# Last down projection of a two-block network: eight subtractions of its activation sums move from VectorE to GpSimd

## The chip, the cores and the metric

The program runs on one core of one Trainium2 chip. The metric is its device time in microseconds (us); the time before is 1531.18 us, the median of three runs (1530.91 to 1531.45). One core has five engines that work side by side, each in the order of its own program: TensorE (PE), VectorE (DVE), ScalarE (ACT), GpSimd (POOL) and SyncE (SP, which here only starts transfers). They wait for each other by semaphores.

## What is computed

Two residual blocks one after the other, on 512 tokens of width 1024, all in float32. What matters here is the end of the second block, a gated feed-forward layer and its last product:

```
h2 = rmsnorm(x, g_ffn)
x = x + (silu(h2 @ w_ff_gate) * (h2 @ w_ff_up)) @ w_ff_down
return rmsnorm(x, g_final)
```

`w_ff_down` is 2816 x 1024. That last product is the "down projection"; the feed-forward layer of the first block has one too, by another procedure that the change leaves alone.

## The kernel before

**Numbers in two parts.** The kernel keeps a float32 value as a high part (type fp32r, rounded) and a low part (value minus high part). A product of two such values is three matmuls: high by high (L1060), high weight-low by high (L1063), high weight by low activation (L1064), all added up in PSUM. Four of these triples, one per block of 128 rows, make what is below called one form. ScalarE rounds to the high part (all by line L1615), VectorE or GpSimd subtracts to get the low part.

**Strassen-like products.** The down projection has 22 row blocks of 128. Its first part, "standard tiles" (`std_tile`, units 0 to 3 in `STD_UNITS`, 512 tokens wide), runs plainly on panels of weights that GpSimd splits (`std_split`, L1004, L1005, L1007). Row blocks 0 to 15 of the other output tiles go by seven products of half size instead of eight (`strassen_unit`, forms F1 to F7, each 256 tokens wide). Six such units follow (unit 0 to 5 below), with standard tiles between some of them. TensorE takes the forms of a unit in the order F1, F6, F7, F5, F2, F3, F4.

**Sums of weights.** For each unit GpSimd makes two sums (`add5` L914, `add7` L923) and the low parts of F1, F7, F2 and F4 (`form_lo_of`, L932). VectorE makes `add6` (L2451), `add3` (L2456) and the low parts of F6, F5, F3 (L2462). ScalarE copies a sum to PSUM (`sum_copy`, L1807) and makes all the high parts.

**Sums of activations.** Before unit 0 the sums of activations must be made, once, for eight k (0 to 7), while TensorE is still on the standard tiles. For each k, ScalarE copies two activations into PSUM (`down_copies`, L2137 and L2138), VectorE adds their low parts (`down_parts`, three instructions L3016 to L3018, the first of which writes the small buffer `down_t1(k)`) and makes four sums (`down_t_sums`, five instructions L3025 to L3029). Three sums stand in PSUM and serve F6, F7, F4: ScalarE rounds them (`down_token_hi`), VectorE subtracts (`down_lo`, L3035). The fourth stands in `down_t1(k)` and serves F5: ScalarE rounds it over the activation itself (`down_token_late`), and VectorE subtracts (`down_late`, L3041, 128x256, both inputs in SBUF). These eight are the late sums of the title of the change.

**What ties them.** `down_t1(k)` is `tmp[:, k % 4 // 2, HALVES[k % 2]]`: four halves of two tiles for eight k. So `down_parts(k)` for k of 4 and more waits until the late low part of k - 4 is made (L3015). `down_parts(5)` also waits for ScalarE's copies of k = 5, which wait for `down_lo(3)`. `sum_copy` of unit 0 waits for `down_lo(5)` (L1802), and so does F1 of unit 0 on TensorE (L1371). F5 of units 0 and 1 waits for the late parts 0 to 3 and 4 to 7, one per triple (L1385). F1 of unit 2 waits for `v`, the third of the joins L3053, L3056, L3059 of the products of units 0 and 1.

**The order of the work** is written out by hand per engine: `down_dve` on VectorE, `pool_down` on GpSimd, `down_act` on ScalarE, `down_strassen` on TensorE. A `std_split` waits on GpSimd until TensorE has begun the panel before (`panel_used`). Low parts of activations, late or not, all count on one semaphore, `t_ready`, in the order `T_ORDER`.

Of the kernel before, what the change touches and what calls it, by code (L numbers as in the profile page):

```python
# [22 lines left out]
KT = D // P  # L23
# [19 lines left out]
QUAD = 4  # L43
# [61 lines left out]
LOADED = 16  # L105
# [132 lines left out]
def build(nc, t, out):  # L238
# [5 lines left out]
    with ctx:  # L244
# [590 lines left out]
        def _(pool):  # L835
# [173 lines left out]
            def pool_down(f):  # L1009

                unit = [pair_of(3 + f, n) for n in range(6)]

                def forms(n, more=None):
                    for form in (F1, F7, F2):
                        form_lo_of(form, unit[n])
                    if more is not None:
                        add5(unit[more])
                        add7(unit[more])
                    form_lo_of(F4, unit[n])

                for u in range(3):
                    for s in range(PAIR):
                        std_split(f, u, s)
                std_split(f, 3, 0)
                add5(unit[0])
                std_split(f, 3, 1)
                add7(unit[0])
                forms(0, 1)
                forms(1, 2)
                forms(2, 3)  # L1030
                forms(3)
                pool.wait_ge(product_done, counted(PRODUCTS, unit[3], F6))
# [21 lines left out]
        def _(pe):  # L1054
# [306 lines left out]
            def strassen_unit(f, p):  # L1361

                j, c = p[1] + 1, p[2]
                last_up = pair_of(f, FT - 1)
                for form in PRODUCTS["later"]:
                    if form in LO_POOL["later"]:
                        pe.wait_ge(form_lo_pool, counted(LO_POOL, p, form))
                    else:
                        pe.wait_ge(form_lo_dve, counted(LO_DVE, p, form))
                    if c == 0 and j == 1 and form in (F1, F6):  # L1370
                        pe.wait_ge(t_ready, t_at(f, "lo", 5 if form == F1 else 4))  # L1371
                    elif c == 0 and form in (F1, F6):
                        pe.wait_ge(joined, down_joined(f, j - 1, "v" if form == F1 else "x"))
                    elif c == 0 and form in (F2, F4) and j == 2:
                        pe.wait_ge(t_ready, t_at(f, "lo", 7))
                        pe.wait_ge(dn_free[f], 1 if form == F2 else 2)
                    elif c == 0 and form in (F2, F4) and j == 3:
                        pe.wait_ge(dn_free[f], 3 if form == F2 else 4)
                    begun = j == 1 and form in (F2, F3, F4)
                    more = j == 2 and form in (F2, F3, F4)  # L1380
                    for k in range(QUAD):
                        if j == 1 and form in (F6, F7, F4):
                            pe.wait_ge(t_ready, t_at(f, "lo", c * QUAD + k))
                        elif j == 1 and form == F5:
                            pe.wait_ge(t_ready, t_at(f, "late", c * QUAD + k))  # L1385
                        sl = slice(k * P, (k + 1) * P)
                        ins = product(down_out(form, p), form_hi(form, p)[:, sl], form_lo(form, p)[:, sl], *down_moving(form, p, k),
                                      c == 0 and k == 0 and form in (F1, F6, F2, F4) and not begun, c == 1 and k == QUAD - 1 and form in (F7, F5, F3, F4) and not more)
                    ins.then_inc(product_done, 1)

            def down_strassen(f):

                for u in range(3):
                    for s in range(PAIR):
# [5 lines left out]
                        ins = std_tile(f, u, s, ps[:, 4 + s, :], start=u == 0, stop=u == 2)  # L1400
                        if u == 2:
                            ins.then_inc(dn_done[f], 1)
                pe.wait_ge(t_ready, t_at(f, "lo", 2))
                for s in range(PAIR):
                    std_tile(f, 3, s, ps[:, 2 + s, :], stop=False).then_inc(part_done, 1)
                for n in range(4):
# [203 lines left out]
        def _(act):  # L1610
# [183 lines left out]
            def sum_copy(p):  # L1794

                act.wait_ge(form_summed, LOADED + turn(p) * 2 + 1)
                if is_first(p):
                    act.wait_ge(merge_ready, 5)
                elif begins(p) and p[0] == 2:
                    act.wait_ge(t_ready, T_MADE[2] + 2 * QUAD)  # L1800
                elif begins(p) and p[0] >= 3:
                    act.wait_ge(t_ready, t_at(p[0] - 3, "lo", 5))  # L1802
                elif begins(p):
                    act.wait_ge(conv_step[0], gate_free_at(pair_of(0, EIGHT - 2)))
                else:
                    act.wait_ge(form_lo_dve, counted(LO_DVE, earlier(p), F3))
# [318 lines left out]
            def down_copies(f, k):  # L2125
# [5 lines left out]
                    act.wait_ge(joined, joined_at(pair_of(f, FT - 1), "u"))  # L2131
                    act.wait_ge(wide_ready[f], FT if k == 2 else b + 1)
                if DOWN_T_AFTER[k] is not None:
                    act.wait_ge(t_ready, t_at(f, "lo", DOWN_T_AFTER[k]))
                if bank == 4:
                    act.wait_ge(dn_free[f], 2)
                do(ps[:, bank, :], f32(wide_hi[:, a, :]), ACT.Identity)  # L2137
# [122 lines left out]
        def _(dve):  # L2260
# [748 lines left out]
            def down_parts(f, k):  # L3009
# [2 lines left out]
                b11, b12, b22 = ps[:, bank, halves[0]], ps[:, bank, halves[1]], ps[:, bank + 1, halves[1]]  # L3012
                dve.wait_ge(gained, LOADED + T_SUMMED[3 + f] + k + 1)
                if k >= 4:
                    dve.wait_ge(t_ready, t_at(f, "late", k - 4))  # L3015
                tt(down_t1(k), b12, f32(wide_lo[:, a, halves[1]]), ADD)  # L3016
                tt(b11, b11, f32(wide_lo[:, a, halves[0]]), ADD)
                link(tt(b22, b22, f32(wide_lo[:, b, halves[1]]), ADD))  # L3018
# [12 lines left out]
            def down_lo(f, k):  # L3031
# [45 lines left out]
            def down_dve(f, residual, add):  # L3077
# [165 lines left out]
```

## Time and profile before

| | before |
|---|---|
| median of three runs | 1531.18 us |
| the profiled execution | 1530.31 us |
| its span, first to last instruction | 1528.5 us |
| busy: PE, DVE, ACT, POOL | 1502.2, 1007.2, 602.2, 1010.6 us |
| granted TensorE clock, mean | 0.996 |
| executed instructions: PE, DVE, ACT, POOL | 9175, 1551, 1079, 801 |

The trace is of the profiled execution; its span begins with the first and ends with the last instruction. All places below are us from the start of the span. The down projection of the second block begins on TensorE at 1397.21, unit 0 at 1435.32, unit 2 at 1458.60. A timeline row gives start and duration; in brackets stands how long the engine had sat idle before the row, and who released it. A row's start is when it was issued; on VectorE and GpSimd an instruction begins a little before the one ahead has ended, so the step from one start to the next is the time that it costs. Idle time of an engine that nobody waits for costs nothing.

### The profile page before, as it was taken

What the parts mean: (1) busy time and instruction counts of PE and PEld (TensorE: products, weight loads), DVE (VectorE), ACT (ScalarE), POOL (GpSimd) and SP (SyncE); (2) the same over time, 40 slices, a digit from 0 to 9 for tenths busy, and PEclk for the clock granted to TensorE, in tenths of its full rate; (3) what the DMA queues carried; (4) which work ended last, traced back from release to release, by engine and by line L of the source; (5) the groups of instructions that cost most, each with busy time, mean ns of one, the idle gap of its engine ahead of it and who ended that gap; (6) DMA issues with size and microseconds to landing.
All of it is one profiled execution on the core that took longest, in us unless ns stands there. A gap on an engine that the chain in (4) does not pass through costs nothing.

```text
span 1528.5 us, 26411 instructions
## 1 busy us (share of the span) xinstructions
PE 1502.2 (98%) x9175; PEld 1349.2 (88%) x9175; DVE 1007.2 (66%) x1551; ACT 602.2 (39%) x1079; POOL 1010.6 (66%) x801
## 2 busy tenths in 40 slices
PE   7999999999999999999999999999999999999998
PEld 6998999998887899988888888888888999999897
DVE  7877777863428477787254665555457787777954
ACT  6543566640113455612032122222235565554542
POOL 4735877766666777766566576576466787776774
PEclk9999999999999999999999999999999999999998
DMA  9942333344233333422323232232232333332332
GB/s 370 402 155 75 104 99 96 110 153 157 98 106 92 94 101 111 120 88 89 101 69 96 68 96 82 81 96 82 69 97 83 97 112 107 97 109 88 101 105 68
DMA packets 235076, 172.89 MB, mean 113 GB/s; under 512 B 5248, under 2 KB 214528, under 8 KB 235008
## 3 DMA queue, kind: packets, MB, share of 16 engines
q1 hardware_dynamic: 235008, 171.98, 36.0%
q8 instruction: 43, 0.70, 0.2%
q14 instruction: 25, 0.20, 0.0%
HBM read 169.86 MB, written 2.10 MB: 112 GB/s over the span
## 4 chain that ended last, share of the span: by engine, by line
PE 58%; DVE 5%; issue 2%; POOL 2%; ACT 1%; DMA 0%; DVEq 0%; POOLq 0%; ACTq 0%
PE ps L1060 19%; PE ps L1064 19%; PE ps L1063 19%; POOL tmp L914 1%; DVE wide_lo L3041 0%; POOL w_lo L932 0%; DMA raw<-in_w_ff_up 0%; POOL tmp L923 0%; DVE act_lo L3035 0%; DVE ps L3027 0%; DVE ps L3028 0%; DVE ps L3029 0%; POOL rope_r L932 0%; DVE tmp L3026 0%; PE ps L1549 0%
## 5 line engine op out<-in xcount | busy, mean ns | idle before, releaser
L900 POOL TENSOR_TENSOR w_lo<-raw,w_hi 128x1024 fp32r<-128x1024 f32 x122 | 305.1, 2501 | 10.2
L1060 PE MATMUL ps<-act_hi,w_hi 128*128 128x256 f32 (+1 forms) x912 | 307.3, 337 | 2.9 <-ACT gates L1867 1.3
L1063 PE MATMUL ps<-act_hi,w_lo 128*128 128x256 f32 (+1 forms) x912 | 303.7, 333 | 0.0
L1064 PE MATMUL ps<-act_lo,w_hi 128*128 128x256 f32 (+1 forms) x912 | 303.7, 333 | 0.0
L1060 PE MATMUL ps<-wide_hi,w_hi 128*128 128x512 f32 (+2 forms) x685 | 247.6, 361 | 2.2 <-DVE tmp L3059 1.2
L1063 PE MATMUL ps<-wide_hi,w_lo 128*128 128x512 f32 (+2 forms) x685 | 246.9, 360 | 0.0
L1064 PE MATMUL ps<-wide_lo,w_hi 128*128 128x512 f32 (+2 forms) x685 | 246.8, 360 | 0.0
L897 POOL TENSOR_TENSOR w_hi<-raw,zero 128x1 fp32r<-128x1 f32 x122 | 31.6, 259 | 281.4 <-PE ps L1060 280.5
L1060 PEld LDWEIGHTS ps<-act_hi,w_hi 128*128 128x128 f32 x912 | 173.9, 191 | 23.4 <-issue 3.2
L1063 PEld LDWEIGHTS ps<-act_hi,w_lo 128*128 128x128 f32 x912 | 173.9, 191 | 17.6 <-issue 1.4
L1064 PEld LDWEIGHTS ps<-act_lo,w_hi 128*128 128x128 f32 x912 | 173.8, 191 | 16.6
L932 POOL TENSOR_TENSOR w_lo<-raw,w_hi 128x512 fp32r<-128x512 f32 x116 | 150.4, 1304 | 53.9 <-ACT w_hi L1615 53.5
L1060 PEld LDWEIGHTS ps<-wide_hi,w_hi 128*128 128x128 f32 x685 | 129.3, 189 | 23.7 <-issue 2.3
L1064 PEld LDWEIGHTS ps<-wide_lo,w_hi 128*128 128x128 f32 x685 | 129.3, 189 | 19.4
L1063 PEld LDWEIGHTS ps<-wide_hi,w_lo 128*128 128x128 f32 x685 | 129.4, 189 | 19.3
L898 POOL TENSOR_SCALAR w_hi<-raw 128x1023 fp32r<-128x1023 f32 x122 | 132.0, 1082 | 0.2 <-issue 0.2
L1615 ACT ACTIVATE w_hi<-ps 128x512 fp32r<-128x512 f32 x116 | 69.0, 595 | 81.8 <-DVE ps L2456 69.3
L1615 ACT ACTIVATE wide_hi<-ps 128x512 fp32r<-128x512 f32 (+2 forms) x94 | 56.6, 606 | 107.6 <-DVE ps L2518 46.8
L932 POOL TENSOR_TENSOR rope_r<-tmp,rope_r 128x512 fp32r<-128x512 f32 x44 | 57.1, 1298 | 60.0 <-ACT rope_r L1615 60.0
L1060 PE MATMUL ps<-gates_r,w_hi 128*128 128x256 f32 x328 | 93.8, 286 | 1.8 <-DVE tmp L2479 1.3
L1060 PE MATMUL ps<-wide_hi 128*128 128x512 f32 (+2 forms) x272 | 91.5, 336 | 3.5 <-DVE wide_lo L2283 2.3
L2462 DVE TENSOR_TENSOR w_lo<-ps,w_hi 128x512 fp32r<-128x512 f32 x116 | 79.6, 686 | 20.9 <-ACT w_hi L1615 18.4
(318 smaller groups left out, 3831.6 us busy)
## 6 DMA issues: line engine op xcount, KB each, us to landing
raw<-in_w_in SPq DMA_DIRECT2D x88, 512.0 KB, 4.0
gates<-in_w_mod_t SPq DMA_DIRECT2D x20, 1024.0 KB, 10.1
raw<-in_w_ffn_up SPq DMA_DIRECT2D x40, 512.0 KB, 3.8
raw<-in_w_ffn_down SPq DMA_DIRECT2D x22, 512.0 KB, 3.6
raw<-in_w_ff_gate SPq DMA_DIRECT2D x22, 512.0 KB, 3.8
raw<-in_w_ff_up SPq DMA_DIRECT2D x22, 512.0 KB, 3.9
raw<-in_w_r_out SPq DMA_DIRECT2D x16, 512.0 KB, 3.5
raw<-in_w_ff_down SPq DMA_DIRECT2D x16, 512.0 KB, 3.7
```

The source lines that it names most:

```text
L897: nc.gpsimd.tensor_tensor(w_hi[:, two, 0:1], raw[:, slot, 0:1], zero[:, :], ADD)
L898: nc.gpsimd.tensor_scalar(w_hi[:, two, 1:], raw[:, slot, 1:], 1.0, 0.0, MUL, ADD).then_inc(hi_made, 1)
L900: nc.gpsimd.tensor_tensor(w_lo[:, two, :], raw[:, slot, :], f32(w_hi[:, two, :]), SUB).then_inc(split_done, 1)
L914: nc.gpsimd.tensor_tensor(sum5(p), v[:, A1], v[:, A2], ADD).then_inc(form_summed, 1)
L932: nc.gpsimd.tensor_tensor(form_lo(form, p), src, f32(form_hi(form, p)), SUB).then_inc(form_lo_pool, 1)
L1060: ins = mm(o, w, a, start=start, stop=False)
L1063: mm(o, wl, a, start=False, stop=False)
L1064: return mm(o, w, al, start=False, stop=stop)
L1615: do(dst, src, ACT.Identity, **how).then_inc(made, 1)
L2462: tt(form_lo(form, p), src, f32(form_hi(form, p)), SUB).then_inc(form_lo_dve, 1)
```

## The change

The eight `down_late` leave VectorE. GpSimd gets them (`token_late`), on a semaphore of their own (`t_late_ready`, the old `fnet_hi_made` reused, which stands at 8 by then, so late part k is number 8 + k + 1). `t_ready` now counts the `down_lo` alone (`t_lo_at`). All that waited for a late part now waits for the new semaphore: F5 on TensorE, `down_parts(k)` for k of 4 and more on VectorE, and the square of tile 0 on ScalarE. ScalarE's order and all transfers stay.

```diff
+def t_lo_at(f, k):
+    return T_MADE[3 + f] + k + 1
...
+        t_late_ready = fnet_hi_made
...
+                def token_late(k):
+
+                    pool.wait_ge(t_hi_made, LOADED + t_at(f, "late", k))
+                    hi, lo = (w[:, down_rows(k)[0], halves[1]] for w in (wide_hi, wide_lo))
+                    nc.gpsimd.tensor_tensor(lo, down_t1(k), f32(hi), SUB).then_inc(t_late_ready, 1)
...
                 std_split(f, 3, 0)
                 add5(unit[0])
+                token_late(0)
                 std_split(f, 3, 1)
                 add7(unit[0])
-                forms(0, 1)
-                forms(1, 2)
+                for k in range(1, 4):
+                    token_late(k)
+                for form in (F1, F7):
+                    form_lo_of(form, unit[0])
+                token_late(4)
+                form_lo_of(F2, unit[0])
+                add5(unit[1])
+                add7(unit[1])
+                form_lo_of(F4, unit[0])
+                token_late(5)
+                form_lo_of(F1, unit[1])
+                token_late(6)
+                form_lo_of(F7, unit[1])
+                token_late(7)
+                form_lo_of(F2, unit[1])
+                add5(unit[2])
+                add7(unit[2])
+                form_lo_of(F4, unit[1])
...
                         elif j == 1 and form == F5:
-                            pe.wait_ge(t_ready, t_at(f, "late", c * QUAD + k))
+                            pe.wait_ge(t_late_ready, KT + c * QUAD + k + 1)
...
                 if k >= 4:
-                    dve.wait_ge(t_ready, t_at(f, "late", k - 4))
+                    dve.wait_ge(t_late_ready, KT + k - 3)
...
-            def down_late(f, k):
-
-                dve.wait_ge(t_hi_made, LOADED + t_at(f, "late", k))
-                hi, lo = (w[:, down_rows(k)[0], halves[1]] for w in (wide_hi, wide_lo))
-                tt(lo, down_t1(k), f32(hi), SUB).then_inc(t_ready, 1)
...
                     down_lo(f, k - 1)
-                    if k >= 3:
-                        down_late(f, k - 3)
                 for m in range(2):
                     dve.wait_ge(dn_done[f], m + 1)
                     residual(m)
                 down_lo(f, 5)
-                down_late(f, 3)
-                dve.wait_ge(t_ready, t_at(f, "lo", 5))
+                dve.wait_ge(t_ready, t_lo_at(f, 5))
```

The other five `down_late` are taken out of `down_dve` in the same way.

**VectorE, behind the sums of k = 3.** The rows are `down_lo(2)`, late part 0 and the first of `down_parts(4)`; `dft_loaded1` is the semaphore `t_hi_made`, `mod_early_loaded3` ScalarE's copies, `fnet_hi_made` the late parts. Before:

```order
L3035 TENSOR_TENSOR gates_r<-ps,gates_r 128x768 [waits dft_loaded1]
L3041 TENSOR_TENSOR wide_lo<-tmp,wide_hi 128x256 [waits dft_loaded1]
L3016 TENSOR_TENSOR tmp<-ps,wide_lo 128x256 [waits t_ready,mod_early_loaded3]
L3017 TENSOR_TENSOR ps<-ps,wide_lo 128x256
```

And changed:

```order
L3065 TENSOR_TENSOR gates_r<-ps,gates_r 128x768 [waits dft_loaded1]
L3046 TENSOR_TENSOR tmp<-ps,wide_lo 128x256 [waits fnet_hi_made,mod_early_loaded3]
L3047 TENSOR_TENSOR ps<-ps,wide_lo 128x256
```

The subtraction is gone, and the first instruction of `down_parts(4)` waits for GpSimd's semaphore in place of VectorE's own.

**GpSimd, from `add5` of unit 0 on.** L914 is `add5`, L923 `add7`, L1004 to L1007 `std_split(3, 1)`, then F1, F7, F2 of unit 0. Before:

```order
L914 TENSOR_TENSOR tmp<-raw 128x512 [waits raw_loaded3]
L1004 TENSOR_TENSOR w_hi<-raw,zero 128x1 [waits panel_used,raw_loaded1]
L1005 TENSOR_SCALAR w_hi<-raw 128x767
L1007 TENSOR_TENSOR w_lo<-raw,w_hi 128x768 [waits hi_made]
L923 TENSOR_TENSOR tmp<-raw 128x512 [waits raw_loaded3,raw_loaded2]
L932 TENSOR_TENSOR w_lo<-raw,w_hi 128x512 [waits x_loaded2]
L932 TENSOR_TENSOR rope_r<-tmp,rope_r 128x512 [waits x_loaded2,x_loaded1]
L932 TENSOR_TENSOR gates_r<-raw,gates_r 128x512 [waits x_loaded2]
L914 TENSOR_TENSOR tmp<-raw 128x512 [waits x_loaded2,raw_loaded1]
```

And changed (the same lines are L919, L928, L1009 to L1012, L937; L1032 is a late part):

```order
L919 TENSOR_TENSOR tmp<-raw 128x512 [waits raw_loaded3]
L1032 TENSOR_TENSOR wide_lo<-tmp,wide_hi 128x256 [waits dft_loaded1]
L1009 TENSOR_TENSOR w_hi<-raw,zero 128x1 [waits panel_used,raw_loaded1]
L1010 TENSOR_SCALAR w_hi<-raw 128x767
L1012 TENSOR_TENSOR w_lo<-raw,w_hi 128x768 [waits hi_made]
L928 TENSOR_TENSOR tmp<-raw 128x512 [waits raw_loaded3,raw_loaded2]
L1032 TENSOR_TENSOR wide_lo<-tmp,wide_hi 128x256 [waits dft_loaded1] x3
L937 TENSOR_TENSOR w_lo<-raw,w_hi 128x512 [waits x_loaded2]
L937 TENSOR_TENSOR rope_r<-tmp,rope_r 128x512 [waits x_loaded2,x_loaded1]
L1032 TENSOR_TENSOR wide_lo<-tmp,wide_hi 128x256 [waits dft_loaded1]
```

Late part 0 stands behind `add5` and in front of the split of the last standard panel; late parts 1 to 3 stand between `add7` and F1 of unit 0; late part 4 ahead of F2.

**GpSimd, from F4 of unit 0 on.** The rows are F4 of unit 0, F1, F7, F2 of unit 1, then the two sums of unit 2. Before:

```order
L932 TENSOR_TENSOR w_lo<-raw,w_hi 128x512 [waits x_loaded2] x2
L932 TENSOR_TENSOR rope_r<-tmp,rope_r 128x512 [waits x_loaded2,x_loaded1]
L932 TENSOR_TENSOR gates_r<-raw,gates_r 128x512 [waits x_loaded2]
L914 TENSOR_TENSOR tmp<-raw 128x512 [waits x_loaded2,raw_loaded3]
L923 TENSOR_TENSOR tmp<-raw 128x512 [waits x_loaded3,raw_loaded3,raw_loaded2]
```

And changed:

```order
L937 TENSOR_TENSOR w_lo<-raw,w_hi 128x512 [waits x_loaded2]
L1032 TENSOR_TENSOR wide_lo<-tmp,wide_hi 128x256 [waits dft_loaded1]
L937 TENSOR_TENSOR w_lo<-raw,w_hi 128x512 [waits x_loaded2]
L1032 TENSOR_TENSOR wide_lo<-tmp,wide_hi 128x256 [waits dft_loaded1]
L937 TENSOR_TENSOR rope_r<-tmp,rope_r 128x512 [waits x_loaded2,x_loaded1]
L1032 TENSOR_TENSOR wide_lo<-tmp,wide_hi 128x256 [waits dft_loaded1]
L937 TENSOR_TENSOR gates_r<-raw,gates_r 128x512 [waits x_loaded2]
L919 TENSOR_TENSOR tmp<-raw 128x512 [waits x_loaded2,raw_loaded3]
L928 TENSOR_TENSOR tmp<-raw 128x512 [waits x_loaded3,raw_loaded3,raw_loaded2]
```

Late parts 5, 6 and 7 stand in front of F1, F7 and F2 of unit 1, and so ahead of the sums of unit 2.

## Rows read from the trace of the kernel before

**Rows 1.** The page, part 1: engine, busy us (share of the span), count.
```profile
PE 1502.2 (98%) x9175; PEld 1349.2 (88%) x9175; DVE 1007.2 (66%) x1551; ACT 602.2 (39%) x1079; POOL 1010.6 (66%) x801
```

**Rows 2.** Timeline of TensorE: start us, duration us, instruction, [idle before, released by].
```profile
1435.32 0.28 PE L1060 MATMUL ps<-wide_hi,w_hi 128*128 128x256 f32 x1
...
1436.75 0.28 PE L1060 MATMUL ps<-gates_r,w_hi 128*128 128x256 f32 x1
...
1451.08 0.39 PE L1060 MATMUL ps<-wide_hi,gates_r 128*128 128x256 f32 x1 [0.27 <-DVE wide_lo L3041]
...
1452.49 0.39 PE L1060 MATMUL ps<-wide_hi,gates_r 128*128 128x256 f32 x1 [0.80 <-DVE wide_lo L3041]
...
1458.60 0.36 PE L1060 MATMUL ps<-wide_hi,w_hi 128*128 128x256 f32 x1 [1.17 <-DVE tmp L3059]
```

**Rows 3.** Timeline of VectorE, down stage, same columns.
```profile
1418.46 0.41 DVE L3041 TENSOR_TENSOR wide_lo<-tmp,wide_hi 128x256 fp32r<-128x256 f32 x1
1418.98 0.42 DVE L3016 TENSOR_TENSOR tmp<-ps,wide_lo 128x256 f32<-128x256 f32 x1
...
1424.22 0.42 DVE L3016 TENSOR_TENSOR tmp<-ps,wide_lo 128x256 f32<-128x256 f32 x1 [0.64 <-ACT ps L2138]
...
1428.40 0.62 DVE L3041 TENSOR_TENSOR wide_lo<-tmp,wide_hi 128x256 fp32r<-128x256 f32 x1
1428.94 1.27 DVE L3169 TENSOR_TENSOR res<-ps,res 128x512 f32<-128x512 f32 x2
...
1431.01 1.27 DVE L3041 TENSOR_TENSOR wide_lo<-tmp,wide_hi 128x256 fp32r<-128x256 f32 x1
1432.20 0.68 DVE L2451 TENSOR_TENSOR ps<-ps,raw 128x512 f32<-128x512 f32 x1
...
1440.46 0.69 DVE L2462 TENSOR_TENSOR w_lo<-ps,w_hi 128x512 fp32r<-128x512 f32 x1 [0.87 <-ACT w_hi L1615]
```

**Rows 4.** Timeline of GpSimd, down stage, same columns.
```profile
1423.61 0.19 POOL L1004 TENSOR_TENSOR w_hi<-raw,zero 128x1 fp32r<-128x1 f32 x1 [1.16 <-PE ps L1060]
...
1426.51 1.28 POOL L914 TENSOR_TENSOR tmp<-raw 128x512 f32<-128x512 f32 x1
1427.75 0.19 POOL L1004 TENSOR_TENSOR w_hi<-raw,zero 128x1 fp32r<-128x1 f32 x1
...
1430.69 1.30 POOL L923 TENSOR_TENSOR tmp<-raw 128x512 f32<-128x512 f32 x1
1432.41 1.30 POOL L932 TENSOR_TENSOR w_lo<-raw,w_hi 128x512 fp32r<-128x512 f32 x1 [0.42 <-ACT w_hi L1615]
```

**Rows 5.** Timeline of ScalarE, down stage, same columns.
```profile
1431.18 0.60 ACT L1807 ACTIVATE ps<-tmp 128x512 f32<-128x512 f32 x1
1431.72 0.62 ACT L1615 ACTIVATE w_hi<-raw 128x512 fp32r<-128x512 f32 x1
...
1445.20 0.41 ACT L1615 ACTIVATE wide_hi<-tmp 128x256 fp32r<-128x256 f32 x1
...
1453.13 0.60 ACT L1807 ACTIVATE ps<-tmp 128x512 f32<-128x512 f32 x1 [2.25 <-DVE w_lo L2462]
```

**Rows 6.** Line L3041 (duration ns min/median/max, first and last start).
```profile
L3041 DVE TENSOR_TENSOR wide_lo<-tmp,wide_hi x8: 414/984/1522, 1418.5 to 1450.9; 128x256 fp32r<-128x256 f32 x8
```

**Rows 7.** Line L1050, same columns.
```profile
L1050 POOL TENSOR_TENSOR gates<-gates,tmp x6: 717/726/727, 1519.4 to 1523.7; 128x256 f32<-128x256 f32 x6
```

**Rows 8.** Timeline of GpSimd, end of the program.
```profile
1519.43 2.09 POOL L1050 TENSOR_TENSOR gates<-gates,tmp 128x256 f32<-128x256 f32 x3 [8.79 <-ACT tmp L2117]
```

**Rows 9.** Stages: us, busy PE, PEld, DVE, ACT, POOL (count), granted clock, DMA share, GB/s.
```profile
52.00:54.00 2.00, 2.00 (x12) 2.00 (x12) 1.73 (x4) 1.16 (x3) 2.00 (x2) 0.56 1.03 386
```

**Rows 10.** Timeline of TensorE, early in the program.
```profile
49.06 3.92 PE L1144 MATMUL ps<-tmp,raw 128*128 128x1 f32 x32
...
53.84 0.41 PE L1063 MATMUL ps<-act_hi,w_lo 128*128 128x256 f32 x1
54.05 0.41 PE L1064 MATMUL ps<-act_lo,w_hi 128*128 128x256 f32 x1
```

More of the change, by code:

```diff
@@ L1019, in forms @@
                     form_lo_of(F4, unit[n])
+                halves = HALVES
+                def token_late(k):
+                    pool.wait_ge(t_hi_made, LOADED + t_at(f, "late", k))
+                    hi, lo = (w[:, down_rows(k)[0], halves[1]] for w in (wide_hi, wide_lo))
+                    nc.gpsimd.tensor_tensor(lo, down_t1(k), f32(hi), SUB).then_inc(t_late_ready, 1)
                 for u in range(3):
@@ L1370, in strassen_unit @@
                     if c == 0 and j == 1 and form in (F1, F6):
-                        pe.wait_ge(t_ready, t_at(f, "lo", 5 if form == F1 else 4))
+                        pe.wait_ge(t_ready, t_lo_at(f, 5 if form == F1 else 4))
                     elif c == 0 and form in (F1, F6):
@@ L1374, in strassen_unit @@
                     elif c == 0 and form in (F2, F4) and j == 2:
-                        pe.wait_ge(t_ready, t_at(f, "lo", 7))
+                        pe.wait_ge(t_ready, t_lo_at(f, 7))
                         pe.wait_ge(dn_free[f], 1 if form == F2 else 2)
@@ L1382, in strassen_unit @@
                         if j == 1 and form in (F6, F7, F4):
-                            pe.wait_ge(t_ready, t_at(f, "lo", c * QUAD + k))
+                            pe.wait_ge(t_ready, t_lo_at(f, c * QUAD + k))
                         elif j == 1 and form == F5:
-                            pe.wait_ge(t_ready, t_at(f, "late", c * QUAD + k))
+                            pe.wait_ge(t_late_ready, KT + c * QUAD + k + 1)
                         sl = slice(k * P, (k + 1) * P)
@@ L1402, in down_strassen @@
                             ins.then_inc(dn_done[f], 1)
-                pe.wait_ge(t_ready, t_at(f, "lo", 2))
+                pe.wait_ge(t_ready, t_lo_at(f, 2))
                 for s in range(PAIR):
@@ L1801, in sum_copy @@
                 elif begins(p) and p[0] >= 3:
-                    act.wait_ge(t_ready, t_at(p[0] - 3, "lo", 5))
+                    act.wait_ge(t_ready, t_lo_at(p[0] - 3, 5))
                 elif begins(p):
@@ L2133, in down_copies @@
                 if DOWN_T_AFTER[k] is not None:
-                    act.wait_ge(t_ready, t_at(f, "lo", DOWN_T_AFTER[k]))
+                    act.wait_ge(t_ready, t_lo_at(f, DOWN_T_AFTER[k]))
                 if bank == 4:
@@ L2234, in square_row @@
                 if m == 0:
-                    act.wait_ge(t_ready, t_at(1, "late", 7))
+                    act.wait_ge(t_late_ready, 2 * KT)
                 last_square(m, m, slice(0, T))
@@ L3114, in down_dve @@
                 down_lo(f, 6)
-                down_late(f, 4)
                 lo(F3, 0)
@@ L3121, in down_dve @@
                 lo(F6, 1)
-                down_late(f, 5)
                 lo(F5, 1)
                 add3(unit[1])
-                down_late(f, 6)
-                down_late(f, 7)
                 lo(F3, 1)
```

## The prediction

> **What bounds the kernel now.** I read the page first: TensorE is busy for 1502.2 of 1528.5 us [rows 1], so only work that keeps TensorE waiting can change the time, and of that there is little. Then I went to the timeline of TensorE in the down stage. It runs without a gap through the standard tiles and through unit 0. Inside F5 of unit 1 it sits idle twice, 0.27 and 0.80 us, each time for VectorE's line L3041, which are late low parts (the third and fourth triple, so parts 6 and 7). Ahead of unit 2 it sits idle for 1.17 us for the join `v` [rows 2]. Counted by starts, units 0 and 1 take 1458.60 - 1435.32 = 23.3 us; a form takes 1.43 us there (1435.32 to 1436.75), so fourteen take 20.0, and about 3.2 us are lost [rows 2]. That is all a better order of this stage could win.
>
> Then the timeline of VectorE. It works without a break on the eight k, and the late parts are cheap while GpSimd rests (0.41 us) and dear beside it (0.62, 1.27, at most 1.52 us) [rows 3, 6]. The reader is to see one more thing there: late part 0 is made at 1418.46, and the first instruction of `down_parts(4)`, which overwrites its source, starts at 1418.98 [rows 3]. On VectorE the guard on that buffer cost nothing, since the subtraction stood just ahead.
>
> Last the timeline of GpSimd at the same time. It is in the splits of the standard panels. Each begins when TensorE has begun the panel before, as the wait of 1.16 us in front of 1423.61 shows; `add5` of unit 0 follows at 1426.51 and `std_split(3, 1)` at 1427.75 [rows 4]. The changed order puts late part 0 exactly between these two.
>
> **Taken away.** Eight L3041 on VectorE. The three idle times of TensorE named above come behind them: the first two directly; the third through `sum_copy` of unit 2, which came at 1453.13 behind an idle 2.25 us in which ScalarE waited for VectorE [rows 5]. If nothing else changed, up to 3.2 us would be won.
>
> **Added.** Eight 128x256 subtractions on GpSimd. The trace has the same shape on that engine: three of L1050 in 2.09 us, 0.70 each (0.73 for one alone) [rows 7, 8]. Bounds: 0.41 us, the cheapest that VectorE did it for, and 1.52, the dearest, beside a busy GpSimd [rows 6]. I take 0.70, the same engine and size. The Trainium skill ("GPSIMD Engine Reference", section 4.1, Engine selection) advises against such a move: elementwise work with two inputs is about twice as slow on GpSimd. By it the price would be an estimated 0.8 us and the sum 0.4 us more; the trace agrees in direction, 0.73 against 0.41.
>
> **The new wait.** What decides is when, not how long. Step by step, with times of before:
>
> 1. Late part 0 can start at 1427.75, where the split stood, and is done at 1428.45 [rows 4, 8]. `down_parts(4)` on VectorE, which began at 1418.98 [rows 3], now begins at 1428.5: 9.5 us later. Behind it on VectorE stand the sums of k = 4 to 7, both residual additions, and everything for unit 0. It cannot go ahead of the wait.
> 2. `down_parts(5)` came 5.24 us after `down_parts(4)` (1424.22), because ScalarE's copies of k = 5 came late (0.64 us idle) [rows 3]. So now 1433.75. Late part 1 must be there by then: 1428.45, plus 2.94 for the split (1427.75 to 1430.69), plus 1.24 for `add7` (as 1426.51 to 1427.75), plus 0.70, is 1433.3 [rows 4, 8]. It holds nothing.
> 3. From 1424.22 to the end of `down_lo(5)` (1431.01) went 6.79 us; late part 2 in it cost 0.54 (1428.40 to 1428.94) and is gone [rows 3]. 1433.75 + 6.25 = 1440.0, 9.0 late.
> 4. `sum_copy` of unit 0 started 0.17 behind that (1431.18), F1's high part 0.54 later (1431.72), its low part on GpSimd 0.69 later (1432.41) and took 1.30 [rows 4, 5]. Now 1442.7. TensorE was ready for F1 of unit 0 at 1435.32 [rows 2]: it idles 7.4 us. The split of panel (3, 1), 0.7 us later, may stop TensorE for some 0.3 us before that; it is hidden in this idle time.
> 5. `add6` of unit 0 came at 1432.20, 1.02 behind the start of `sum_copy`, because late part 3 stood there for 1.27 [rows 3, 5]. Without it, it starts 0.62 behind (the copy lasts 0.60), at 1440.8: 8.6 late. From here VectorE and ScalarE hand the k = 6 and 7 to each other. Late part 4 in it saves nothing: VectorE then sat idle 0.87 anyway, at 1440.46, for ScalarE [rows 3]. So ScalarE rounds late part 5 at 1453.8 instead of 1445.20, done at 1454.2 [rows 5]. GpSimd has F1 of unit 1 behind late part 5: 1454.3 + 0.70 + 1.25 (a step of GpSimd at 512 columns) = 1456.25. TensorE, done with unit 0 about 1453, waits again until then.
> 6. GpSimd goes on with late part 6, F7, late part 7, F2, and `add5` of unit 2: 0.70 + 1.25 + 0.70 + 1.25 + 1.25 = 5.15, to 1461.4. `sum_copy` of unit 2 follows at 1461.5, from 1453.13, and from it to unit 2 on TensorE went 5.47 us (1458.60) [rows 2, 5]: 1467.0. By TensorE alone it would be 1456.3 + 10.0 = 1466.3, so the chain over GpSimd ends last by a little.
>
> Sum: unit 2 starts at 1467.0 instead of 1458.6, **8.4 us later**. This contains the gain: both halves of F5's wait are gone, and 9.5 has shrunk by the late parts removed. Behind unit 2 nothing shortens it: TensorE ran without a gap from there to the last panels, so all shifts, the transfers of the last panels too, which start when the units before free their slots. The profiled execution took 1530.31 us, so 1538.7 for its like; the median of the runs shown is 0.87 above it, and my forecast for a median is **1539.6 us**.
>
> **Rivals.**
>
> A. **Faster.** VectorE is not held, because late part 0 is made early enough. The guard costs nothing up to about 1419, and little up to some 2 us more, since F1 of unit 0 had its low part at 1433.7 and TensorE came for it at 1435.32 [rows 2, 4]. Then the three waits go and the time is 1531.2 - 3.2 = 1528 us. For it: the late parts are indeed what TensorE waits for. Against: GpSimd stands behind `panel_used` until 1423.61, and the split and `add5` are in front in its program [rows 4]. 4 in 100.
>
> B. **Most of the hold is absorbed**, the stage having more room than the timeline shows: 1531 to 1536 us. The room that rows show is 1.6 us. 4 in 100, half of it within 0.2%.
>
> C. **The clock.** Early in the trace TensorE did 32 matmuls of one column in 3.92 us, and the granted clock then was 0.56 in 52 to 54, that is mostly the lower of 1.2 and 2.4 GHz; matmuls of 256 columns stepped 0.21 us [rows 9, 10] against 0.12 in a form now (1.43 over twelve) [rows 2]. An idle time of 7.4 us may do the same. In unit 0 this is hidden, since TensorE idles about 3 us again before unit 1. If it falls in unit 1, some 12 to 20 matmuls cost 0.09 more each, 1.1 to 1.8 us, less the 0.7 of room in step 6: up to 1541. The Trainium skill ("TensorE: Matmul & The Clock Gate", Part 1) says that the default is the half rate and that idling brings it back; by that rule the clock falls in the first idle time at least. That it reaches the end: 10 in 100.
>
> D. **GpSimd and VectorE slow each other** as in the rows of L3041, and a late part costs up to 1.52 us. Four of them stand in line (parts 0, 5, 6, 7), 0.82 more each, and late part 1 would then come some 0.4 us late too: 3.7 more, 1543.3. Against: at the time VectorE mostly has one input in PSUM, and GpSimd's own steps hardly grew. 7 in 100.
>
> **How the numbers follow.** My forecast, with the prices of steps 1 to 6 good to about 1 us, has 75 in 100. With a late part at 0.41 the sum is 1.2 less, 1538.4; below that some of the hold would have to be absorbed. The range is 1536.5 to 1543.3, which leaves out A, most of B and little else. A measurement of this kernel can tell about 0.2%, 3 us, from no change. Slower by more: 75 + 10 + 7 + 2 of B, 94 in 100; within: 2; faster: 4.
>
> **What would show it.** In the changed profile: VectorE idle some 9.8 us ahead of the first instruction of `down_parts(4)`, released by GpSimd's late part 0 at 1428.4; TensorE idle about 7 us ahead of unit 0 and about 3 ahead of unit 1, with no waits inside F5 of unit 1; a late part at 0.7 us on GpSimd; unit 2 at 1467. Wrong would be: no idle VectorE at 1418, late part 0 before 1423, or a gap ahead of unit 2 that no GpSimd work explains.

## The result, and the profile after

The changed kernel takes 1539.84 us (median of five runs, 1539.3 to 1540.41) against 1531.18 before (five runs, 1530.8 to 1531.45): 1.0058 times, 95% interval 1.0047 to 1.0069. It is slower by 8.7 us; the prediction said 1539.6. The profiled execution took 1540.41 us.

The page of the changed kernel: eight instructions fewer on VectorE, eight more on GpSimd, the span 9.9 us longer.

```profile
span 1538.4 us, 26411 instructions
...
PE 1505.4 (98%) x9175; PEld 1352.0 (88%) x9175; DVE 1001.1 (65%) x1543; ACT 602.6 (39%) x1079; POOL 1016.2 (66%) x809
```

The profiled executions reach the first standard tile of the down projection at slightly different times, 1397.21 before and 1398.55 now, ahead of everything that was moved; what sets them apart is not known. So stages are compared by length, from the first standard tile on TensorE to F1 of unit 2. Before that was 1458.60 - 1397.21 = 61.39 us [rows 2]. The timeline of TensorE in the changed kernel (start, duration, instruction, idle time before it and releaser; the changed kernel's line numbers are higher by 5 up to the new function on GpSimd, L1032, by 30 behind it, so L1090 is L1060, and by less, 24 at the joins, behind the place where `down_late` was taken out, so L3083 is L3059):

```profile
1398.55 0.40 PE L1090 MATMUL ps<-wide_hi,w_hi 128*128 128x512 f32 x1
...
1444.12 0.58 PE L1090 MATMUL ps<-wide_hi,w_hi 128*128 128x256 f32 x1 [6.95 <-POOL w_lo L937]
...
1457.84 0.39 PE L1090 MATMUL ps<-wide_hi,w_hi 128*128 128x256 f32 x1 [1.39 <-POOL w_lo L937]
...
1468.46 0.36 PE L1090 MATMUL ps<-wide_hi,w_hi 128*128 128x256 f32 x1 [0.28 <-DVE tmp L3083]
```

The length is 1468.46 - 1398.55 = 69.91, 8.52 more. Most of it is one row: 6.95 us of idle time ahead of unit 0, released by GpSimd's low part of F1. Unit 0 begins 45.57 us into the stage, 7.46 later than before (38.11), and units 0 and 1 together take 24.34 us in place of 23.28. The two idle times inside F5 [rows 2] are gone, and that ahead of unit 2 fell from 1.17 to 0.28; a new one of 1.39 us stands ahead of unit 1.

VectorE answers to [rows 3]. Its timeline, from `down_lo(2)` on:

```profile
1418.93 0.95 DVE L3065 TENSOR_TENSOR gates_r<-ps,gates_r 128x768 fp32r<-128x768 f32 x1
1429.91 0.43 DVE L3046 TENSOR_TENSOR tmp<-ps,wide_lo 128x256 f32<-128x256 f32 x1 [10.04 <-POOL wide_lo L1032]
...
1435.15 0.42 DVE L3046 TENSOR_TENSOR tmp<-ps,wide_lo 128x256 f32<-128x256 f32 x1 [0.98 <-ACT ps L2168]
...
1440.53 0.95 DVE L3065 TENSOR_TENSOR act_lo<-ps,act_hi 128x768 fp32r<-128x768 f32 x1
1442.30 0.70 DVE L2481 TENSOR_TENSOR ps<-ps,raw 128x512 f32<-128x512 f32 x1 [0.83 <-ACT ps L1837]
...
1450.58 0.69 DVE L2492 TENSOR_TENSOR w_lo<-ps,w_hi 128x512 fp32r<-128x512 f32 x1 [1.49 <-ACT w_hi L1645]
...
1463.67 0.70 DVE L2481 TENSOR_TENSOR ps<-ps,raw 128x512 f32<-128x512 f32 x1 [3.57 <-ACT ps L1837]
```

The second row is the point: VectorE sat idle for 10.04 us ahead of the first instruction of `down_parts(4)`, released by L1032, GpSimd's late part. Before it followed late part 0 at once. Below it: `down_parts(5)`, `down_lo(5)`, `add6` of unit 0, the low part of F3 (idle 1.49 for ScalarE, where it had been 0.87), and `add6` of unit 2.

GpSimd answers to [rows 4]:

```profile
1424.95 0.19 POOL L1009 TENSOR_TENSOR w_hi<-raw,zero 128x1 fp32r<-128x1 f32 x1 [1.16 <-PE ps L1090]
...
1427.83 1.29 POOL L919 TENSOR_TENSOR tmp<-raw 128x512 f32<-128x512 f32 x1
1429.07 0.74 POOL L1032 TENSOR_TENSOR wide_lo<-tmp,wide_hi 128x256 fp32r<-128x256 f32 x1
1429.77 0.19 POOL L1009 TENSOR_TENSOR w_hi<-raw,zero 128x1 fp32r<-128x1 f32 x1
...
1442.80 1.27 POOL L937 TENSOR_TENSOR w_lo<-raw,w_hi 128x512 fp32r<-128x512 f32 x1 [2.28 <-ACT w_hi L1645]
...
1455.81 0.74 POOL L1032 TENSOR_TENSOR wide_lo<-tmp,wide_hi 128x256 fp32r<-128x256 f32 x1 [1.91 <-ACT wide_hi L1645]
1456.51 1.28 POOL L937 TENSOR_TENSOR w_lo<-raw,w_hi 128x512 fp32r<-128x512 f32 x1
...
1461.64 1.31 POOL L919 TENSOR_TENSOR tmp<-raw 128x512 f32<-128x512 f32 x1
```

Late part 0 stands between `add5` and the split of panel (3, 1), starts the moment `add5` lets it, and releases VectorE. The rows from 1455.81 are late part 5, F1 of unit 1, and `add5` of unit 2. ScalarE, to [rows 5], rounds late part 5 and copies the sum of unit 2:

```profile
1455.33 0.41 ACT L1645 ACTIVATE wide_hi<-tmp 128x256 fp32r<-128x256 f32 x1
...
1462.98 0.60 ACT L1837 ACTIVATE ps<-tmp 128x512 f32<-128x512 f32 x1 [3.09 <-POOL tmp L919]
```

One late part on GpSimd, all eight alike:

```profile
L1032 POOL TENSOR_TENSOR wide_lo<-tmp,wide_hi x8: 729/740/752, 1429.1 to 1459.7; 128x256 fp32r<-128x256 f32 x8
```

### The profile page after: what moved, and what is told of

The parts are those of the page before. It is cut to its first block, busy times and chain, and to the rows that moved or that the text cites. A ratio compares the mean times of both kernels' runs of the same rounds, so it can differ in the third digit from the quotient of the medians.

```text
span 1538.4 us, 26411 instructions
## 1 busy us (share of the span) xinstructions
PE 1505.4 (98%) x9175; PEld 1352.0 (88%) x9175; DVE 1001.1 (65%) x1543; ACT 602.6 (39%) x1079; POOL 1016.2 (66%) x809
## 4 chain that ended last, share of the span: by engine, by line
PE 59%; DVE 3%; POOL 3%; issue 2%; ACT 1%; DMA 1%; DVEq 0%; POOLq 0%; ACTq 0%
PE ps L1090 20%; PE ps L1093 19%; PE ps L1094 19%; POOL tmp L919 1%; DMA raw<-in_w_ff_up 1%; POOL w_lo L937 0%; POOL tmp L928 0%; POOL rope_r L937 0%; POOL w_lo L1012 0%; PE ps L1579 0%; POOL w_lo L905 0%; DVE gates L3216 0%; ACT wide_hi L1645 0%; PE ps L1371 0%; POOL wide_lo L1032 0%
## 5 line engine op out<-in xcount | busy, mean ns | idle before, releaser
L1090 PE MATMUL ps<-act_hi,w_hi 128*128 128x256 f32 (+1 forms) x912 | 308.0, 338 | 2.9 <-ACT gates L1897 1.3
L1090 PE MATMUL ps<-wide_hi,w_hi 128*128 128x512 f32 (+2 forms) x685 | 248.6, 363 | 9.7 <-POOL w_lo L937 8.3
L1090 PEld LDWEIGHTS ps<-act_hi,w_hi 128*128 128x128 f32 x912 | 174.6, 191 | 23.3 <-issue 3.2
L937 POOL TENSOR_TENSOR w_lo<-raw,w_hi 128x512 fp32r<-128x512 f32 x116 | 150.3, 1304 | 52.4 <-ACT w_hi L1645 52.0
L1090 PEld LDWEIGHTS ps<-wide_hi,w_hi 128*128 128x128 f32 x685 | 129.8, 190 | 32.2 <-POOL w_lo L937 9.0
L1645 ACT ACTIVATE wide_hi<-ps 128x512 fp32r<-128x512 f32 (+2 forms) x94 | 56.6, 606 | 107.5 <-DVE ps L2548 46.8
L1090 PE MATMUL ps<-gates_r,w_hi 128*128 128x256 f32 x328 | 94.2, 287 | 1.9 <-DVE tmp L2509 1.3
L1090 PE MATMUL ps<-wide_hi 128*128 128x512 f32 (+2 forms) x272 | 91.3, 336 | 3.3 <-DVE wide_lo L2313 1.6
L937 POOL TENSOR_TENSOR rope_r<-tmp,rope_r 128x512 fp32r<-128x512 f32 x44 | 57.2, 1301 | 56.2 <-ACT rope_r L1645 56.2
```

Of the source, the lines that this page charges most:

```text
L937: nc.gpsimd.tensor_tensor(form_lo(form, p), src, f32(form_hi(form, p)), SUB).then_inc(form_lo_pool, 1)
L1090: ins = mm(o, w, a, start=start, stop=False)
L1645: do(dst, src, ACT.Identity, **how).then_inc(made, 1)
```

## The experiments

Theory W: the loss is the hold of VectorE by the place of late part 0 (and 1) in GpSimd's order. Rival P: it is the price of the subtractions on GpSimd, and of two engines sharing SBUF. Rival C: TensorE's half rate after the idle time makes up a good part. "Stage" is the length defined above, read from the one profiled execution of each kernel; behind it stand its two ends. What follows F1 of unit 2, up to the end of the span, takes 69.8 to 70.2 us in all ten kernels, so the stage holds nearly all of what the changes do. The medians of before were 1530.76 beside the first four kernels and 1530.74 beside the last four.

| kernel | median us | ratio (95%) | stage us (from, to) | stage less before |
|---|---|---|---|---|
| before | 1531.18 | | 61.39 (1397.21, 1458.60) | |
| changed | 1539.84 | 1.0058 (1.0047 to 1.0069) | 69.91 (1398.55, 1468.46) | +8.52 |
| wait alone | 1539.08 | 1.0054 (1.0040 to 1.0069) | 69.81 (1397.35, 1467.16) | +8.42 |
| late 0 on VectorE | 1538.41 | 1.0050 (1.0036 to 1.0064) | 68.79 (1397.66, 1466.45) | +7.40 |
| late 0, 1 on VectorE | 1531.67 | 1.0005 (0.9995 to 1.0014) | 61.05 (1398.04, 1459.09) | -0.34 |
| each twice | 1543.77 | 1.0084 (1.0069 to 1.0098) | 73.51 (1397.69, 1471.20) | +12.12 |
| 0, 1 early | 1531.19 | 1.0002 (0.9992 to 1.0011) | 61.05 (1398.52, 1459.57) | -0.34 |
| all placed | 1527.83 | 0.9981 (0.9972 to 0.9990) | 58.26 (1397.88, 1456.14) | -3.13 |
| filled | 1540.85 | 1.0063 (1.0050 to 1.0077) | 70.94 (1398.02, 1468.96) | +9.55 |
| 5, 6, 7 only | 1529.62 | 0.9992 (0.9983 to 1.0001) | 60.25 (1397.31, 1457.56) | -1.14 |

### The wait alone

The kernel before, no work moved, one wait added:

```diff
 def down_parts(f, k):
+    if k == 4:
+        dve.wait_ge(form_summed, LOADED + turn(pair_of(3 + f, 0)) * 2 + 1)
     if k >= 4:
         dve.wait_ge(t_ready, t_at(f, "late", k - 4))
```

> The kernel before, all eight late parts on VectorE, with one wait added: the first instruction of down_parts(4) waits for GpSimd's add5 of unit 0. Theory W (the loss is the hold of VectorE by where GpSimd stands): VectorE idles about 9 us there, F1 of unit 0 starts at about 1442, the time is 8.0 to 9.0 us above before, about 1539.8. Rival P (the loss is the price of the subtractions on GpSimd and of two engines sharing SBUF): no work was moved, so 1531.2, within 0.5 us of before. Rival C (TensorE's half rate makes up a good part): TensorE still idles and falls to the lower clock, but the loss should then be smaller where the idle time is shorter; the two are told apart by the granted clock against the starts of unit 1 and unit 2.

VectorE (late part 0, then the first instruction of `down_parts(4)`) and TensorE (F1 of unit 0, F1 of unit 2):

```profile
1418.60 0.41 DVE L3043 TENSOR_TENSOR wide_lo<-tmp,wide_hi 128x256 fp32r<-128x256 f32 x1
1428.01 0.42 DVE L3018 TENSOR_TENSOR tmp<-ps,wide_lo 128x256 f32<-128x256 f32 x1 [9.00 <-POOL tmp L914]
```

```profile
1442.56 0.58 PE L1060 MATMUL ps<-wide_hi,w_hi 128*128 128x256 f32 x1 [6.94 <-POOL w_lo L932]
...
1467.16 0.36 PE L1060 MATMUL ps<-wide_hi,w_hi 128*128 128x256 f32 x1 [1.18 <-DVE tmp L3061]
```

ScalarE, `sum_copy` of unit 2:

```profile
1461.69 0.60 ACT L1807 ACTIVATE ps<-tmp 128x512 f32<-128x512 f32 x1 [2.25 <-DVE w_lo L2462]
```

The wait costs 9.00 us on VectorE, 6.94 ahead of unit 0 and 8.42 in the stage. With all eight subtractions still on VectorE, a loss of the full size is there. P falls as the main cause. This kernel speaks against C too, although the clock fell here as well (granted 0.50 from 1442 to 1446): `sum_copy` of unit 2 waits for VectorE as before [rows 5] and comes 64.34 us into the stage in place of 55.92, 8.42 later, and TensorE again sits idle ahead of unit 2, for 1.18 us. So VectorE's delay alone sets the 8.42. That the changed kernel lost nearly the same (8.52) is partly chance: it has no more waits in F5 and no long one ahead of unit 2, but pays instead for the late parts that stand in line on GpSimd (below).

### Late part 0 alone back on VectorE

```diff
                     down_lo(f, k - 1)
+                    if k == 3:
+                        down_late(f, 0)
...
                 add5(unit[0])
-                token_late(0)
                 std_split(f, 3, 1)
                 add7(unit[0])
+                pool.wait_ge(t_late_ready, KT + 1)
                 for k in range(1, 4):
```

> The changed kernel with late part 0 alone back on VectorE. Theory W: late part 1, behind the split of panel (3, 1) and add7 on GpSimd, is ready at about 1432.7 and takes over the hold, now of down_parts(5), so little is won: 7.0 to 7.8 us above before, about 1538.6. A narrower reading (only the place of late part 0 is at fault) gives 1531 or less. Rival P: one eighth of the loss back, 1538.8.

VectorE (late part 0; `down_parts(5)`), then GpSimd (split of panel (3, 1), `add7`, late parts 1 and 2):

```profile
1418.91 0.41 DVE L3071 TENSOR_TENSOR wide_lo<-tmp,wide_hi 128x256 fp32r<-128x256 f32 x1
...
1433.17 0.42 DVE L3046 TENSOR_TENSOR tmp<-ps,wide_lo 128x256 f32<-128x256 f32 x1 [9.47 <-POOL wide_lo L1032]
```

```profile
1428.19 0.20 POOL L1009 TENSOR_TENSOR w_hi<-raw,zero 128x1 fp32r<-128x1 f32 x1
...
1431.08 1.29 POOL L928 TENSOR_TENSOR tmp<-raw 128x512 f32<-128x512 f32 x1
1432.33 1.43 POOL L1032 TENSOR_TENSOR wide_lo<-tmp,wide_hi 128x256 fp32r<-128x256 f32 x2
```

The added wait on GpSimd keeps the count of the semaphore in order. The hold moved from k = 4 to k = 5 and is 9.47 us long. Only 1.1 us of the stage came back. So it is not late part 0 as such: late part 1, behind the last split, does it too when part 0 is out of the way. P's number (1538.8) is as near here; the next kernel parts them.

### Late parts 0 and 1 back on VectorE

As above, with `if k in (3, 4): down_late(f, k - 3)` on VectorE, and `pool.wait_ge(t_late_ready, KT + 2)` and `range(2, 4)` on GpSimd.

> The changed kernel with late parts 0 and 1 back on VectorE, 2 to 7 on GpSimd where the change has them. Theory W: no hold is left. Unit 0 starts on time at 1435.3, unit 1 about 1.8 us late (F1 of unit 1 behind late part 5 on GpSimd), no waits in F5 of unit 1, unit 2 at about 1458.2: 1530.3 to 1531.3, about 1530.9. Rival P: six eighths of the loss stay, about 1537.7.

TensorE (F1 of unit 1, F1 of unit 2), then GpSimd (late part 5, F1 of unit 1):

```profile
1448.48 0.39 PE L1090 MATMUL ps<-wide_hi,w_hi 128*128 128x256 f32 x1 [2.10 <-POOL w_lo L937]
...
1459.09 0.36 PE L1090 MATMUL ps<-wide_hi,w_hi 128*128 128x256 f32 x1 [0.28 <-DVE tmp L3089]
```

```profile
1446.47 0.73 POOL L1032 TENSOR_TENSOR wide_lo<-tmp,wide_hi 128x256 fp32r<-128x256 f32 x1 [1.92 <-ACT wide_hi L1645]
1447.15 1.27 POOL L937 TENSOR_TENSOR w_lo<-raw,w_hi 128x512 fp32r<-128x512 f32 x1
```

VectorE, ahead of `down_parts(6)`:

```profile
1433.56 0.43 DVE L3046 TENSOR_TENSOR tmp<-ps,wide_lo 128x256 f32<-128x256 f32 x1 [0.66 <-POOL wide_lo L1032]
```

With two of eight moved back, the long hold is gone and the stage 0.34 us shorter than before; against the expectation, 0.66 us is left ahead of `down_parts(6)`. Unit 1 waits 2.10 us for its F1, which stands behind late part 5 on GpSimd: a loss of order that the changed kernel has too (1.39 us, there with a slower unit 0 in front). The median, 1531.67, is 0.8 above the expected one and 0.4 above the range given; the interval holds both no change and the 0.34 us.

### Each late part made twice

```diff
-nc.gpsimd.tensor_tensor(lo, down_t1(k), f32(hi), SUB).then_inc(t_late_ready, 1)
+nc.gpsimd.tensor_tensor(lo, down_t1(k), f32(hi), SUB).then_inc(late_once, 1)
+pool.wait_ge(late_once, k + 1)
+nc.gpsimd.tensor_tensor(lo, down_t1(k), f32(hi), SUB).then_inc(t_late_ready, 1)
```

> The changed kernel with every late part made twice on GpSimd, the second time behind a semaphore of the first (same result). Each costs about 1.45 us instead of 0.70. Theory W: four of them stand in line (0, 5, 6, 7) and late part 1 comes about 0.4 us late besides, so 3.0 to 3.7 us above the changed kernel, about 1543.2. Rival P (the price is the loss): the loss doubles, about 1548.5.

F1 of units 0, 1 and 2 on TensorE:

```profile
1444.48 0.58 PE L1093 MATMUL ps<-wide_hi,w_hi 128*128 128x256 f32 x1 [7.41 <-POOL w_lo L938]
...
1459.00 0.58 PE L1093 MATMUL ps<-wide_hi,w_hi 128*128 128x256 f32 x1 [2.19 <-POOL w_lo L938]
...
1471.20 0.36 PE L1093 MATMUL ps<-wide_hi,w_hi 128*128 128x256 f32 x1 [0.35 <-DVE tmp L3086]
```

Twice the price costs 3.6 us in the stage, 3.9 in the median. One more price of each of the eight is thus worth less than half of the 8.7 us, about as W had it (3.0 to 3.7, four in line), and the loss does not double. But it is not nothing. A second subtraction added 0.80 us to a step of GpSimd here; if the first, at 0.70, counts alike, about 3.1 us of the changed kernel's stage are its price, an estimate. The idle time of 2.19 us ahead of unit 1 was followed by the lower clock in unit 1 (last section); it stayed hidden, since TensorE still sat idle for 0.35 us ahead of unit 2, for the join.

### Late parts 0 and 1 early, all eight on GpSimd

```diff
                 for u in range(3):
                     for s in range(PAIR):
+                        if (u, s) == (2, 1):
+                            token_late(0)
                         std_split(f, u, s)
+                token_late(1)
                 std_split(f, 3, 0)
                 add5(unit[0])
-                token_late(0)
                 std_split(f, 3, 1)
                 add7(unit[0])
-                for k in range(1, 4):
+                for k in range(2, 4):
```

> All eight late parts on GpSimd as in the changed kernel; only 0 and 1 stand earlier, in the pauses in which GpSimd waits for TensorE (0 ahead of the split of panel (2, 1), 1 ahead of that of (3, 0)). Theory W: VectorE is never held, unit 0 starts on time, unit 1 about 1.1 to 1.9 us late behind late part 5 and F1 on GpSimd. From the first standard tile to unit 2 on TensorE 60.0 to 61.0 us (61.39 before, 69.91 changed); time about 1530.3, 0.5 to 1.4 us under before. Rival P (the price on GpSimd is the loss): all eight are still there, so at least 1538.

The one wait of VectorE for a late part that is left, ahead of `down_parts(6)`:

```profile
1434.05 0.43 DVE L3048 TENSOR_TENSOR tmp<-ps,wide_lo 128x256 f32<-128x256 f32 x1 [1.19 <-POOL wide_lo L1032]
```

Two instructions moved into pauses of GpSimd take 8.9 us out of the stage of the changed kernel. It is 0.05 us above the range that was given. I had not priced this: late part 2, behind `add7`, holds `down_parts(6)` for 1.19. Late part 5 then starts on GpSimd 48.44 us into the stage, against 47.24 in the next kernel, which does not have this hold. The median is 0.9 above the expected 1530.3 and no different from before.

### All late parts placed

On top of that, GpSimd's order from the split of panel (3, 1) on is: late 2, `add7`, late 3, F1, F7, F2, `add5` and `add7` of unit 1, late 4, F4, then F1 of unit 1, late 5, F7, late 6, late 7, `add5` of unit 2, F2, `add7`, F4.

> As e5_early01, and late parts 2 to 7 placed where GpSimd has time: 4 ahead of F4 of unit 0, 5 behind F1 of unit 1, 6 and 7 behind F7, with add5 of unit 2 ahead of F2 of unit 1. Theory W: no wait of TensorE is left in units 0 to 2. From the first standard tile to unit 2 58.3 to 59.3 us; time 1528.0 to 1529.3, about 2.5 us under before. Rival P: at least 1538.

F1 of units 1 and 2 on TensorE, with no idle time before them:

```profile
1446.06 0.28 PE L1091 MATMUL ps<-wide_hi,w_hi 128*128 128x256 f32 x1
...
1456.14 0.28 PE L1091 MATMUL ps<-wide_hi,w_hi 128*128 128x256 f32 x1
```

From 1446.06 to 1456.14 are 10.08 us, and the stage is 3.13 us shorter than before: nearly all that the prediction counted as lost (3.2) [rows 2]. Stage and median are both a little under the ranges given (58.3 to 59.3; 1528.0 to 1529.3). 1527.83 us is the fastest version of the study, 2.9 us under the kernel before measured beside it and 12.0 under the changed one, with the same instructions as the latter.

### TensorE filled

```diff
+def fill(f, n):
+    pe.wait_ge(t_ready, t_lo_at(f, 4))
+    for i in range(n):
+        mm(ps[:, 7, 0:HALF], wide_hi[:, 20, 0:P], wide_hi[:, 21, 0:HALF], start=True, stop=True)
...
+                fill(f, 30)
                 for n in range(4):
                     strassen_unit(f, pair_of(3 + f, n))
```

> The changed kernel; TensorE does 30 needless matmuls of 256 columns into a free half bank (result unused) in its idle time ahead of unit 0. Rival C: the half rate after that idle time costs the path some 1 to 2 us, so the time falls to about 1538. Theory W: the granted clock stays at 1.0, unit 0 ends about 2 us earlier, and the idle time ahead of unit 1 grows from 1.39 to about 3.3 us by as much; the time stays within 0.5 us of the changed kernel, 1539.8.

In the changed kernel the clock fell in the idle time ahead of unit 0, which began at 1437.2. The windows, two us each (busy PE, PEld, DVE, ACT, POOL; then the granted clock, DMA share and GB/s):

```profile
1440.00:1442.00 2.00, 0.00 (x0) 0.00 (x0) 1.48 (x3) 1.33 (x3) 0.52 (x1) 0.96 0.00 0
1442.00:1444.00 2.00, 0.00 (x0) 0.00 (x0) 1.69 (x4) 1.62 (x4) 1.20 (x1) 0.50 0.00 0
1444.00:1446.00 2.00, 1.88 (x9) 1.88 (x10) 1.88 (x4) 1.22 (x3) 1.36 (x2) 0.50 0.00 0
1446.00:1448.00 2.00, 2.00 (x11) 2.00 (x11) 1.92 (x4) 1.06 (x2) 0.00 (x0) 0.50 0.00 0
1448.00:1450.00 2.00, 2.00 (x16) 2.00 (x16) 1.09 (x2) 0.94 (x4) 1.86 (x2) 0.83 0.00 0
```

With the filling TensorE did this (30 matmuls in one row, F1 of unit 1, F1 of unit 2), at these clocks:

```profile
1438.95 3.86 PE L1395 MATMUL ps<-wide_hi 128*128 128x256 f32 x30 [2.31 <-DVE act_lo L3072]
...
1457.30 0.39 PE L1090 MATMUL ps<-wide_hi,w_hi 128*128 128x256 f32 x1 [2.22 <-POOL w_lo L937]
...
1468.96 0.28 PE L1090 MATMUL ps<-wide_hi,w_hi 128*128 128x256 f32 x1
```

```profile
1444.00:1446.00 2.00, 2.00 (x19) 2.00 (x19) 1.86 (x6) 0.70 (x2) 1.14 (x1) 1.00 0.00 0
1456.00:1458.00 2.00, 0.70 (x5) 0.70 (x6) 1.73 (x3) 1.84 (x5) 2.00 (x4) 0.93 0.17 49
1458.00:1460.00 2.00, 2.00 (x11) 2.00 (x11) 0.85 (x2) 1.12 (x2) 2.00 (x3) 0.50 0.00 0
1460.00:1462.00 2.00, 2.00 (x14) 2.00 (x14) 0.00 (x0) 0.00 (x0) 2.00 (x2) 0.72 0.00 0
```

The clock stayed at 1.00 through unit 0, and unit 1 began at 1457.30 - 1398.02 = 59.28 us into the stage; in the changed kernel it was 1457.84 - 1398.55 = 59.29. So the half rate in unit 0 cost the path nothing, and C falls. The idle time ahead of unit 1 grew, by less than expected (2.83 us in all, not 3.3) and in two pieces (0.61 ahead of F4 of unit 0, 2.22 ahead of unit 1), and now the clock fell there: 0.50 in 1458 to 1460. From F1 of unit 1 to F1 of unit 2 went 11.66 us, against 10.62 in the changed kernel. That is the missing 1 us, and TensorE is now what ends last: there is no idle time ahead of unit 2. 1540.85 was outside the 0.5 us that was expected.

### Late parts 5, 6 and 7 only

Late parts 0 to 4 on VectorE as before; on GpSimd late 5 behind F1 of unit 1, 6 behind F7, 7 behind F2.

> Late parts 0 to 4 on VectorE where they were before, 5, 6 and 7 on GpSimd, each behind a form of unit 1 (F1, F7, F2). Theory W: no hold, no wait in F5, the wait ahead of unit 2 stays for the most part (about 1.4 us). From the first standard tile to unit 2 60.0 to 60.6 us; time about 1530.0, 1 us under before. Rival P: three eighths of the loss, 1534.

```profile
1457.56 0.36 PE L1082 MATMUL ps<-wide_hi,w_hi 128*128 128x256 f32 x1 [1.24 <-DVE tmp L3081]
```

The stage is 60.25, as forecast; the wait ahead of unit 2, 1.24 us, is about the one of before (1.17). The median is 1.1 us under before, with an interval that just holds no change. GpSimd helps where VectorE was late, and the rest of the gain needs the copy of the sum of unit 2 earlier, which "all placed" has.

## Why the prediction was right

Its steps, counted from the first standard tile (1397.21 before, 1398.55 now):

| step | predicted | measured |
|---|---|---|
| 1. `down_parts(4)` | 31.3 | 1429.91: 31.36 |
| 2. `down_parts(5)` | 36.5 | 1435.15: 36.60 |
| 4. F1 of unit 0 | 45.5 | 1444.12: 45.57 |
| 5. F1 of unit 1 | 59.0 | 1457.84: 59.29 |
| 6. F1 of unit 2 | 69.8 | 1468.46: 69.91 |

- **Step 1**, the place: right, and shown by the wait alone and by the early 0 and 1. Late part 0 came right behind `add5`, and VectorE idled 10.04 us.
- **The price**: 0.70 us taken, 1429.77 - 1429.07 = 0.70 measured, 740 ns for one (median). Neither bound came near. The Trainium skill ("GPSIMD Engine Reference", section 4.1) has two-input work at about twice VectorE's time. The trace agrees roughly: 740 against 414 ns, VectorE's cheapest, is 1.8 times [rows 6].
- **Steps 2 and 3**: right. Late part 1 held nothing as long as part 0 did; taken from behind it, it held by itself, as the experiment with late part 0 shows.
- **Step 4**: F1 of unit 0 came 0.1 later than worked out. The step put the delay of TensorE by the later split at some 0.3 us; its last standard matmuls came 0.35 later in the stage than before, and as foreseen the idle time hides it.
- **Step 5**: F1 of unit 1 0.3 later than worked out. ScalarE's rounding at 1455.33 is 56.78 into the stage, 56.6 predicted, and late part 5 and F1 follow.
- **Step 6**: `sum_copy` of unit 2 at 1462.98, 64.43 into the stage; predicted 64.3. The chain to unit 2 took 5.48 us, as before (5.47).
- **The gain inside the loss**: right. Both waits in F5 are gone; "all placed" shows that they and the third are worth 3.1 us when nothing else stands in the way.
- **Rival A** (VectorE not held) did not happen, and its price was too good. With the long hold gone and GpSimd's order else as in the change, the time was 1531.19 (0 and 1 early), not 1528: it had left out that F1 of unit 1 stands behind late part 5, 2.11 us ahead of unit 1 there. That "all placed" came to 1527.83 took a new order of the other late parts as well.
- **Rival B** (most of the hold absorbed) did not happen: `down_parts(4)` began 9.59 us later in the stage than before (31.36 against 21.77), and unit 2 8.52.
- **Rival C**: the clock fell ahead of unit 0, and the idle time before unit 1 was 1.39 us, not about 3, since unit 0 ran slower. That was foreseen as hidden, and it was. The Trainium skill ("TensorE: Matmul & The Clock Gate", Part 1) says idling brings back the half rate; the trace agrees, 0.50 at 1442 to 1448. But the 1.39 us did not bring it down in unit 1 (1.00 from 1458 on). The way in which it does reach the end was seen in the filled kernel.
- **Rival D**: did not happen. GpSimd's late parts took 729 to 752 ns.
- **The number**: the stage is 8.52 us longer, 8.4 worked out. The profiled execution took 1540.41 us where 1538.7 was given for its like; 1.34 of these 1.7 lie ahead of the stage (1398.55 against 1397.21). The forecast for the median does not carry them, and the median hit it within 0.3.

## What to carry to other kernels

A guard on a small reused buffer is free while its reader stands just ahead of its writer on the same engine; move the reader to another engine, and the writer, with all behind it, waits for everything that stands in front of the reader there. So price a move by the time at which the new engine comes to it, and put it in a pause of that engine: here the same eight instructions gave 8.7 us of loss or 2.9 us of gain by their places alone. After taking one hold away, look for the next in the same guard (here k = 5 behind k = 4) before judging the move.

## What was not expected of the hardware

TensorE fell to half rate in unit 1 of the filled kernel after idle times of only 0.61 and 2.22 us, which ended at 1453.39 and 1457.30, with matmuls in between; in the changed kernel a single one of 1.39 us at the same place did not do it. Needless matmuls that kept the clock up in one stage so lost about 1 us in the next. Both idle times are not always needed: with each late part made twice, a single one of 2.19 us, which ended at 1459.00, was followed by the same fall,

```profile
1460.00:1462.00 2.00, 2.00 (x12) 2.00 (x11) 0.47 (x1) 0.26 (x1) 2.00 (x3) 0.50 0.03 8
```

while single ones of 2.10 and 2.11 us at the same place (late 0 and 1 on VectorE; 0 and 1 early) were followed by 1.00 throughout. What decides between these was not tried.
